# Expert feed-forward in pairs of column steps: weight pieces of 2 row tiles by 1024 columns, scatter into the T and Y banks

## The chip, the core and the metric

The kernel runs on one core of a Trainium2 chip. The metric is the device time of one execution in microseconds. The kernel before takes 1410.08 us (median of 3 runs, 1409.67 to 1410.91).

## What is computed

The program is a two-layer encoder trunk for 256 tokens of width 1024, all in float32. The first layer is a Fourier mixer and a dense SwiGLU; the second is neighbourhood attention and a top-2-of-8 expert SwiGLU. The change touches only the experts:

```python
def expert_block(args):            # xb: the tokens routed to expert e
    xb, e = args
    return (jax.nn.silu(xb @ w_gate[e]) * (xb @ w_up[e])) @ w_down[e]
# w_gate, w_up: 8 x 1024 x 3584;  w_down: 8 x 3584 x 1024
y = ys[dest] * g_sorted[:, None]
out = jnp.zeros((T, D)).at[tok_sorted].add(y)
```

## The kernel before

**Split products.** Each float32 product is made of three matmuls of a reduced type: a number is written as hi + lo, and `three` (L1059) issues hi*hi, hi*lo and lo*hi. Weights come from HBM in pieces of 1 MB (128 partitions by 2048 values, `PIECE`). SyncE (SP) issues one DMA for each into one of 7 raw buffers (`load`, L305), as soon as VectorE (DVE) is done with the buffer's last content. ScalarE (ACT) copies the piece to `w_hi` (`split_hi`, L394), DVE subtracts to `w_lo` (`split_lo`, L671), and TensorE (PE) multiplies (12 matmuls of 512 columns for a piece: three for each of its 4 blocks of 128 by 512). There are only three `w_hi`/`w_lo` buffers (`SPLIT`), so ACT may split piece j+3 only when PE has ended piece j, which PE tells by the semaphore `piece_used`.

**An expert** has 42 pieces. Its hidden width of 3584 is worked in 7 steps of 512 columns (`STEPS`). For each step: gate, 2 pieces of 4 row tiles by 512 columns, into a PSUM bank G[c % 2] (`columns`, L1393); up, 2 pieces, into U[c % 2]; then the down product of the step before, 2 pieces, into the two Y banks (`down`, L1421). ACT takes the Silu of G (`silu`, L597), DVE multiplies it by U (`hidden`, L944), PE transposes the result in four blocks into T[c % 2] (`hidden_transposes`, L1411), and ACT and DVE make hi and lo of it (`hidden_hi`, L603, `hidden_rest`, L951). The function `expert_pieces` (L95) writes the order of the pieces out by hand, and `expert` of ACT (L617) and of DVE (L978) walk through that list: at piece j they first do the small work that hangs on it, then split piece j+3. An engine works strictly in this order.

**Around an expert.** While the last pieces of expert E run, PE gathers the tokens of expert E+1 (`gather`, L1372, 8 matmuls into G[1] and U[1]) and transposes them (`transpose_tokens`, L1384). Then it runs the two pieces of the next expert's first gate step (`first_gate`, L1405), and only then the scatter of expert E: 8 matmuls (L1480, L1481) into T[0], G[1], T[1] and U[1], which DVE adds to h (`add_result`, L968, L974). Experts 0 to 6 are one hardware loop (`Fori`) on each engine, with the same instructions in each round; the eighth stands behind it. In the loop each round of ACT begins at piece 1 of the list, and the first activation of the round is the Silu of step 0.

Of the kernel before, what the change touches and what calls it, by code (L numbers as in the profile page):

```python
# [30 lines left out]
KD = D // P  # L31
# [61 lines left out]

STEPS = FFE // BANK
def expert_pieces():  # L95

    order = []
    for c in range(STEPS):
        order += [("gate", c, 0), ("gate", c, 1), ("up", c, 0), ("up", c, 1)]
        if c:  # L100
            order += [("down", c - 1, 0), ("down", c - 1, 1)]
    order += [("down", STEPS - 1, 0), ("down", STEPS - 1, 1)]
    return order, {x: j for j, x in enumerate(order)}
# [10 lines left out]
def expert_source(ewg, ewu, ewd, e, j):  # L114

    kind, c, half = EXPERT[j]
    v = {"gate": ewg, "up": ewu, "down": ewd}[kind][0].rearrange("e (k p) n -> p (e k) n", p=P)
    if kind == "down":
        return v[:, bass.ds(e * (FFE // P) + (BANK // P * c + KROW * half), KROW), :], KROW, D
    return v[:, bass.ds(e * KD + KH * half, KH), BANK * c:BANK * (c + 1)], KH, BANK  # L120


def trunk(nc, x, norm_mix, norm_ffn, w_in, w_out, w_qkv, w_o, ffg, ffu, ffd, router_w, router_b,
# [149 lines left out]
    def has_before(j, E, back):  # L273

        return E is not None or j >= back


    TY = [T[0], T[1], Y[0], Y[1]]
# [112 lines left out]
    def _(act):  # L391
# [205 lines left out]
        def silu(E, c):  # L597
            act.wait_ge(piece_used, piece(AT["gate", c, 1], E))
            if c != 1:
                act.wait_ge(e_hid, E * STEPS + max(c - 1, 0))  # L600
            nc.scalar.activation(silu_g[c % 2][:], G[c % 2][:], ACT.Silu).then_inc(e_silu, 1)
# [15 lines left out]
        def expert(E, ahead):  # L617

            for j, (kind, c, half) in enumerate(EXPERT):
                if j < AHEAD - SPLIT:  # L620
                    continue
                if (kind, half) == ("gate", 1):
                    silu(E, c)
                    if c:
                        hidden_hi(E, c - 1)
                if (kind, c, half) == ("up", STEPS - 1, 1) and ahead:
                    gather_copy(E + 2)
                if (kind, c, half) == ("down", STEPS - 2, 0):
                    if ahead:
                        gather_hi(E + 2)  # L630
                    hidden_hi(E, STEPS - 1)
                if (kind, c, half) == ("down", STEPS - 1, 1):
                    result_hi(E)
                if ahead or j + SPLIT < PER_EXPERT:
                    split_hi(j + SPLIT, E)
            if ahead:
                for j in range(PER_EXPERT + SPLIT, PER_EXPERT + AHEAD):
                    split_hi(j, E)
# [22 lines left out]
    def _(dve):  # L661
# [282 lines left out]
        def hidden(E, c):  # L944
            dve.wait_ge(e_silu, E * STEPS + (c + 1))
            dve.wait_ge(piece_used, piece(AT["up", c, 1], E))
            if c != 1:
                dve.wait_ge(e_hidT, E * STEPS + max(c - 1, 0))
            nc.vector.tensor_tensor(hid[c % 2][:], U[c % 2][:], silu_g[c % 2][:], ALU.mult).then_inc(e_hid, 1)
# [18 lines left out]
        def add_result(E, e):  # L968
            for b in range(NB):
                for q in range(2):  # L970
                    dve.wait_ge(e_scatter, NB * (2 * E + q) + b + 1)
                    part = h[:, b, BANK * q:BANK * (q + 1)]
                    src = T[q] if b == 0 else (G, U)[q][1]
                    last = nc.vector.scalar_tensor_tensor(out=part, in0=src[:], scalar=mo["weight"][:, b, bass.ds(e, 1)],  # L974
                                                          in1=part, op0=ALU.mult, op1=ALU.add)
                last.then_inc(e_added, 1)

        def expert(E, sweep, ahead):  # L978

            e = E - NE if sweep else E  # L980
            for j, (kind, c, half) in enumerate(EXPERT):
                if j < AHEAD - SPLIT:
                    continue
                if (kind, half) == ("gate", 1) and c:
                    hidden_rest(E, c - 1)
                if (kind, half) == ("up", 1):
                    hidden(E, c)
                    if c == 0:
                        next_selection(E, e, sweep, ahead)
                    if c == STEPS - 1 and ahead:  # L990
                        gather_copy(E + 2)
                if (kind, c, half) == ("down", STEPS - 2, 0):
                    if ahead:
                        gather_lo(E + 2)
                    hidden_rest(E, STEPS - 1)
                if (kind, c, half) == ("down", STEPS - 1, 1):
                    result_rest(E)
                if ahead or j + SPLIT < PER_EXPERT:
                    split_lo(j + SPLIT, E)
# [51 lines left out]
    def _(pe):  # L1051
# [340 lines left out]

        def columns(E, kind, c, bk):  # L1393
            for half in range(2):
                j = AT[kind, c, half]
                ready(j, E)
                if (kind, c) == ("gate", 0):
                    pe.wait_ge(e_xlo, 2 * E + half + 1)
                wh, wl = parts(j, E, KH)
                for k in range(KH):  # L1400
                    kk = KH * half + k
                    last = three(bk[:], mo["xg_hi"][:, kk], mo["xg_lo"][:, kk], wh[:, k], wl[:, k], kk == 0, kk == KD - 1)
                last.then_inc(piece_used, 1)

        def first_gate(E):  # L1405

            pe.wait_ge(e_silu, E * STEPS)
            columns(E, "gate", 0, G[0])

        def expert(E, ahead):  # L1410
# [29 lines left out]

            for c in range(STEPS):
                if c:
                    if c >= 2:
                        pe.wait_ge(e_silu, E * STEPS + (c - 1))
                    columns(E, "gate", c, G[c % 2])
                    hidden_transposes(c - 1)
                if c != 1:
                    pe.wait_ge(e_hid, E * STEPS + max(c - 1, 0))
                columns(E, "up", c, U[c % 2])
                if c == 0:  # L1450
                    pe.wait_ge(e_added, NB * E)
# [3 lines left out]
                    last.then_inc(e_selT, 1)  # L1455
                if 1 <= c < STEPS - 1:
                    down(c - 1, 0)
                    down(c - 1, 1)

            pe.wait_ge(e_hid, E * STEPS + (STEPS - 1))  # L1460
            if ahead:
                pe.wait_ge(e_sel, E + 2)
                gather()
            down(STEPS - 2, 0)
            if ahead:
                transpose_tokens(E + 2)
            hidden_transposes(STEPS - 1)
            down(STEPS - 2, 1)
            down(STEPS - 1, 0)
# [5 lines left out]
            for q in range(2):  # L1475
                pe.wait_ge(e_ylo, 2 * E + 1 + q)
                for b in range(NB):
                    cs = slice(BANK * q, BANK * (q + 1))
                    bk = T[q] if b == 0 else (G, U)[q][1]
                    nc.tensor.matmul(bk[:], mo["selT"][:, b], mo["y_hi"][:, cs], start=True, stop=False)  # L1480
# [66 lines left out]
```

## Time and profile before

| | us |
|---|---|
| median of 3 runs | 1410.08 |
| the execution that was profiled | 1411.13 |
| its span, first to last instruction | 1409.3 |
| one expert in the loop, from the timeline | 122.4 |
| PE busy in the span | 1388.9 |
| DVE busy in the span | 1127.1 |
| ACT busy in the span | 926.1 |

The span is the time between the first and the last instruction; the profiled execution's own time is 1.8 us longer. PE is the engine of the matmuls; its records overlap (one record is 0.39 us long, and the next starts 0.23 us after it), so the start-to-start time is what a matmul costs. On ACT and DVE, too, an instruction starts some 0.1 us before the record of the one ahead of it ends.

### The profile page before, as it was taken

To read this page: it belongs to the slowest core of one execution; us is meant where nothing else is said; L and a number is where in the kernel's file an instruction comes from. 1 tells how busy PE (TensorE), PEld (TensorE's weight loads), DVE (VectorE), ACT (ScalarE), POOL (GpSimd) and SP (SyncE) were. 2 spreads that over 40 slices of the span, in tenths; PEclk is the share of its full clock that TensorE was granted. 3 is DMA by queue.
4 is the path that set the end of the run, shared out by engine and by line. 5 is a ranking of instruction groups with operands and counts; after the bars stand their busy time and mean duration, and the time that the engine had idled before them with its cause. 6 is when DMAs were issued, how large, how long until landed. Compare 5 with 4: busy or idle time off the path is not lost.

```text
span 1409.3 us, 17766 instructions
## 1 busy us (share of the span) xinstructions
PE 1388.9 (99%) x6511; PEld 1151.1 (82%) x6511; DVE 1127.1 (80%) x811; ACT 926.1 (66%) x760; POOL 20.0 (1%) x29
## 2 busy tenths in 40 slices
PE   9999999999979999999999999999999999999997
PEld 8888888787868888888888888888888888888885
DVE  6455666655668889888988988898898889889887
ACT  6353444444656777777777777777777777777774
POOL 0000000000030000000000000000000000000000
PEclk9999999999989999999999999999999999999999
DMA  9367775563148999999999999999999999999992
GB/s 356 132 179 221 220 202 179 172 198 109 32 140 313 361 375 340 359 377 354 356 362 375 334 362 374 357 357 376 366 329 377 363 354 350 368 375 333 372 375 90
DMA packets 191689, 420.10 MB, mean 298 GB/s; under 512 B 19168, under 2 KB 21344, under 8 KB 191648
## 3 DMA queue, kind: packets, MB, share of 16 engines
q1 hardware_dynamic: 178432, 415.00, 81.9%
q10 hardware_dynamic: 12784, 3.26, 1.7%
q0 software_dynamic: 432, 1.28, 0.3%
q8 instruction: 27, 0.44, 0.1%
q14 instruction: 14, 0.11, 0.0%
HBM read 418.47 MB, written 1.05 MB: 298 GB/s over the span
## 4 chain that ended last, share of the span: by engine, by line
PE 97%; DVE 1%; ACT 1%; DMA 1%; issue 0%; POOL 0%; POOLq 0%; SPq 0%; DVEq 0%; ACTq 0%
PE bank_G L1061 10%; PE bank_G L1063 10%; PE bank_G L1062 10%; PE bank_U L1061 10%; PE bank_U L1063 10%; PE bank_U L1062 10%; PE bank_Y L1061 8%; PE bank_Y L1063 8%; PE bank_Y L1062 8%; PE bank_T L1418 2%; PE bank_G L1310 1%; PE bank_T L1061 1%; PE bank_T L1063 1%; PE bank_T L1062 1%; PE bank_T L1321 1%; PE bank_G L1379 1%
## 5 line engine op out<-in xcount | busy, mean ns | idle before, releaser
L674 DVE TENSOR_TENSOR w_lo<-raw,w_hi 128x2048 fp32r<-128x2048 f32 x390 | 888.0, 2290 | 197.7 <-ACT w_hi L400 197.6
L400 ACT ACTIVATE w_hi<-raw 128x2048 fp32r<-128x2048 f32 x390 | 748.2, 1919 | 284.3 <-PE bank_U L1063 102.1
L1061 PE MATMUL bank_Y<-w_hi,hidT_hi 128*128 128x512 f32 x492 | 192.3, 391 | 0.0
L1063 PE MATMUL bank_Y<-w_hi,hidT_lo 128*128 128x512 f32 x492 | 191.6, 389 | 0.0
L1062 PE MATMUL bank_Y<-w_lo,hidT_hi 128*128 128x512 f32 x492 | 191.4, 389 | 0.0
L1061 PE MATMUL bank_U<-w_hi,xg_hi 128*128 128x512 f32 x448 | 179.1, 400 | 0.0
L1061 PE MATMUL bank_G<-w_hi,xg_hi 128*128 128x512 f32 x448 | 175.7, 392 | 0.7 <-DVE w_lo L674 0.5
L1063 PE MATMUL bank_U<-w_hi,xg_lo 128*128 128x512 f32 x448 | 175.0, 391 | 0.0
L1063 PE MATMUL bank_G<-w_hi,xg_lo 128*128 128x512 f32 x448 | 174.8, 390 | 0.0
L1062 PE MATMUL bank_G<-w_lo,xg_hi 128*128 128x512 f32 x448 | 174.7, 390 | 0.0
L1062 PE MATMUL bank_U<-w_lo,xg_hi 128*128 128x512 f32 x448 | 174.6, 390 | 0.0
L1063 PEld LDWEIGHTS bank_Y<-w_hi,hidT_lo 128*128 128x128 f32 x492 | 92.3, 188 | 19.4
L1061 PEld LDWEIGHTS bank_Y<-w_hi,hidT_hi 128*128 128x128 f32 x492 | 92.4, 188 | 19.2
L1062 PEld LDWEIGHTS bank_Y<-w_lo,hidT_hi 128*128 128x128 f32 x492 | 92.4, 188 | 18.7
L1061 PEld LDWEIGHTS bank_G<-w_hi,xg_hi 128*128 128x128 f32 x448 | 84.3, 188 | 18.5 <-DVE w_lo L674 0.8
L1063 PEld LDWEIGHTS bank_U<-w_hi,xg_lo 128*128 128x128 f32 x448 | 84.1, 188 | 18.2
L1063 PEld LDWEIGHTS bank_G<-w_hi,xg_lo 128*128 128x128 f32 x448 | 84.4, 188 | 17.7
L1062 PEld LDWEIGHTS bank_G<-w_lo,xg_hi 128*128 128x128 f32 x448 | 84.4, 188 | 17.3
L1062 PEld LDWEIGHTS bank_U<-w_lo,xg_hi 128*128 128x128 f32 x448 | 84.3, 188 | 16.3
L1061 PEld LDWEIGHTS bank_U<-w_hi,xg_hi 128*128 128x128 f32 x448 | 84.2, 188 | 16.0
L1061 PE MATMUL bank_G<-w_hi,act_hi 128*128 128x512 f32 (+1 forms) x176 | 67.4, 383 | 2.8 <-DVE act_lo L699 1.4
L1061 PE MATMUL bank_U<-w_hi,act_hi 128*128 128x512 f32 (+1 forms) x176 | 67.7, 385 | 0.0
(264 smaller groups left out, 1471.1 us busy)
## 6 DMA issues: line engine op xcount, KB each, us to landing
raw<-in_expert_w_gate SPq DMA_DIRECT2D x112, 1024.0 KB, 7.0
raw<-in_expert_w_up SPq DMA_DIRECT2D x112, 1024.0 KB, 7.0
raw<-in_expert_w_down SPq DMA_DIRECT2D x112, 1024.0 KB, 6.8
raw<-in_nat_w_qkv SPq DMA_DIRECT2D x12, 1024.0 KB, 5.1
raw<-in_ffn_w_gate SPq DMA_DIRECT2D x11, 1024.0 KB, 7.9
raw<-in_ffn_w_up SPq DMA_DIRECT2D x11, 1024.0 KB, 6.0
raw<-in_ffn_w_down SPq DMA_DIRECT2D x11, 1024.0 KB, 5.2
raw<-in_fourier_w_in SPq DMA_DIRECT2D x4, 1024.0 KB, 11.5
```

The source lines that it names most:

```text
L400: nc.scalar.activation(w_hi[w][:], raw[s][:], ACT.Copy).then_inc(hi_made, 1)
L674: nc.vector.tensor_tensor(w_lo[w][:], raw[s][:], w_hi[w][:].bitcast(f32), ALU.subtract).then_inc(lo_made, 1)
L1061: nc.tensor.matmul(out_, xh, wh, start=start, stop=False)
L1062: nc.tensor.matmul(out_, xh, wl, start=False, stop=False)
L1063: return nc.tensor.matmul(out_, xl, wh, start=False, stop=stop)
L1310: last = nc.tensor.matmul(G[i % 2][:, S * n:S * (n + 1)], att["qT"][p0:p0 + HD, m, P * b:P * (b + 1)], att["kT"][p0:p0 + HD, m, :], start= ...
L1321: last = nc.tensor.transpose(T[g % 2][:, o:o + P], hid[g % 2][:, S * n + P * k:S * n + P * (k + 1)], ident[:])
L1379: last = nc.tensor.matmul((G, U)[q][1][:], mo["sel"][:, b], mo[part][:, b, BANK * q:BANK * (q + 1)], start=(n == 0), stop=(n == len(terms) ...
L1418: last = nc.tensor.transpose(T[c % 2][:, P * k:P * (k + 1)], hid[c % 2][:, P * k:P * (k + 1)], ident[:])
```

## The change

The seven steps are grouped as three pairs and a single one (`PAIRED`). A gate or up piece of a pair is 2 row tiles by 1024 columns in place of 4 by 512, so a pair has 4 gate pieces, then 4 up pieces, and each piece feeds both G banks (or both U banks). The number of pieces, their size and the number of matmuls stay. The down products of a pair come after the up pieces of the next one. The first two of the four gate pieces of the first pair stand ahead of the scatter, the other two behind it. The scatter goes into T[0], Y[0], T[1] and Y[1], since G[1] then holds a gate sum. ACT takes the two Silus and the two `hidden_hi` of a pair together behind the last gate piece; DVE does the same with its part. Token transposes stand now between the pieces of down step 4 and the last hidden transposes behind them.

```diff
--- before.py
+++ after.py
@@ -92,14 +92,20 @@
 
 
 STEPS = FFE // BANK
+PAIRED = [(0, 1), (2, 3), (4, 5), (6,)]
+assert sum(PAIRED, ()) == tuple(range(STEPS))
+def parts_of(p):
+
+    return 2 * len(PAIRED[p])
+
 def expert_pieces():
 
     order = []
-    for c in range(STEPS):
-        order += [("gate", c, 0), ("gate", c, 1), ("up", c, 0), ("up", c, 1)]
-        if c:
-            order += [("down", c - 1, 0), ("down", c - 1, 1)]
-    order += [("down", STEPS - 1, 0), ("down", STEPS - 1, 1)]
+    for p in range(len(PAIRED)):
+        order += [(kind, p, part) for kind in ("gate", "up") for part in range(parts_of(p))]
+        if p:
+            order += [("down", c, half) for c in PAIRED[p - 1] for half in range(2)]
+    order += [("down", c, half) for c in PAIRED[-1] for half in range(2)]
     return order, {x: j for j, x in enumerate(order)}
 
 
@@ -117,7 +123,9 @@
     v = {"gate": ewg, "up": ewu, "down": ewd}[kind][0].rearrange("e (k p) n -> p (e k) n", p=P)
     if kind == "down":
         return v[:, bass.ds(e * (FFE // P) + (BANK // P * c + KROW * half), KROW), :], KROW, D
-    return v[:, bass.ds(e * KD + KH * half, KH), BANK * c:BANK * (c + 1)], KH, BANK
+    width = BANK * len(PAIRED[c])
+    tiles = PIECE // width
+    return v[:, bass.ds(e * KD + tiles * half, tiles), BANK * PAIRED[c][0]:BANK * PAIRED[c][0] + width], tiles, width
 
 
 def trunk(nc, x, norm_mix, norm_ffn, w_in, w_out, w_qkv, w_o, ffg, ffu, ffd, router_w, router_b,
@@ -274,6 +282,10 @@
 
         return E is not None or j >= back
 
+
+    def group_of(c):
+
+        return [p for p, steps in enumerate(PAIRED) if c in steps][0]
 
     TY = [T[0], T[1], Y[0], Y[1]]
     STREAM = [TY, TY, TY, [G[0], G[1], U[0], Y[0]]]
@@ -595,7 +607,7 @@
                 nc.scalar.activation(mo["xg_hi"][:, 4 * q:4 * q + 4], four((G, U)[q][1]), ACT.Copy).then_inc(e_xhi, 1)
 
         def silu(E, c):
-            act.wait_ge(piece_used, piece(AT["gate", c, 1], E))
+            act.wait_ge(piece_used, piece(AT["gate", group_of(c), parts_of(group_of(c)) - 1], E))
             if c != 1:
                 act.wait_ge(e_hid, E * STEPS + max(c - 1, 0))
             nc.scalar.activation(silu_g[c % 2][:], G[c % 2][:], ACT.Silu).then_inc(e_silu, 1)
@@ -619,15 +631,16 @@
             for j, (kind, c, half) in enumerate(EXPERT):
                 if j < AHEAD - SPLIT:
                     continue
-                if (kind, half) == ("gate", 1):
-                    silu(E, c)
-                    if c:
-                        hidden_hi(E, c - 1)
-                if (kind, c, half) == ("up", STEPS - 1, 1) and ahead:
+                if kind == "gate" and half == parts_of(c) - 1:
+                    for step in PAIRED[c]:
+                        silu(E, step)
+                    for step in PAIRED[c - 1] if c else ():
+                        hidden_hi(E, step)
+                if (kind, c) == ("up", len(PAIRED) - 1) and half == parts_of(c) - 1 and ahead:
                     gather_copy(E + 2)
+                if (kind, c, half) == ("down", STEPS - 3, 0) and ahead:
+                    gather_hi(E + 2)
                 if (kind, c, half) == ("down", STEPS - 2, 0):
-                    if ahead:
-                        gather_hi(E + 2)
                     hidden_hi(E, STEPS - 1)
                 if (kind, c, half) == ("down", STEPS - 1, 1):
                     result_hi(E)
@@ -943,7 +956,7 @@
 
         def hidden(E, c):
             dve.wait_ge(e_silu, E * STEPS + (c + 1))
-            dve.wait_ge(piece_used, piece(AT["up", c, 1], E))
+            dve.wait_ge(piece_used, piece(AT["up", group_of(c), parts_of(group_of(c)) - 1], E))
             if c != 1:
                 dve.wait_ge(e_hidT, E * STEPS + max(c - 1, 0))
             nc.vector.tensor_tensor(hid[c % 2][:], U[c % 2][:], silu_g[c % 2][:], ALU.mult).then_inc(e_hid, 1)
@@ -970,7 +983,7 @@
                 for q in range(2):
                     dve.wait_ge(e_scatter, NB * (2 * E + q) + b + 1)
                     part = h[:, b, BANK * q:BANK * (q + 1)]
-                    src = T[q] if b == 0 else (G, U)[q][1]
+                    src = (T, Y)[q][b]
                     last = nc.vector.scalar_tensor_tensor(out=part, in0=src[:], scalar=mo["weight"][:, b, bass.ds(e, 1)],
                                                           in1=part, op0=ALU.mult, op1=ALU.add)
                 last.then_inc(e_added, 1)
@@ -981,17 +994,19 @@
             for j, (kind, c, half) in enumerate(EXPERT):
                 if j < AHEAD - SPLIT:
                     continue
-                if (kind, half) == ("gate", 1) and c:
-                    hidden_rest(E, c - 1)
-                if (kind, half) == ("up", 1):
-                    hidden(E, c)
+                if kind == "gate" and half == parts_of(c) - 1 and c:
+                    for step in PAIRED[c - 1]:
+                        hidden_rest(E, step)
+                if kind == "up" and half == parts_of(c) - 1:
+                    for step in PAIRED[c]:
+                        hidden(E, step)
                     if c == 0:
                         next_selection(E, e, sweep, ahead)
-                    if c == STEPS - 1 and ahead:
+                    if c == len(PAIRED) - 1 and ahead:
                         gather_copy(E + 2)
+                if (kind, c, half) == ("down", STEPS - 3, 0) and ahead:
+                    gather_lo(E + 2)
                 if (kind, c, half) == ("down", STEPS - 2, 0):
-                    if ahead:
-                        gather_lo(E + 2)
                     hidden_rest(E, STEPS - 1)
                 if (kind, c, half) == ("down", STEPS - 1, 1):
                     result_rest(E)
@@ -1390,22 +1405,29 @@
                     last = nc.tensor.transpose((G, U)[q][1][:, P * k:P * (k + 1)], mo["xg"][:, P * kk:P * (kk + 1)], ident[:])
                 last.then_inc(e_xT, 1)
 
-        def columns(E, kind, c, bk):
-            for half in range(2):
-                j = AT[kind, c, half]
+        def columns(E, kind, p, parts_now):
+
+            banks = [(G if kind == "gate" else U)[c % 2] for c in PAIRED[p]]
+            tiles = KD // parts_of(p)
+            for part in parts_now:
+                j = AT[kind, p, part]
                 ready(j, E)
-                if (kind, c) == ("gate", 0):
-                    pe.wait_ge(e_xlo, 2 * E + half + 1)
-                wh, wl = parts(j, E, KH)
-                for k in range(KH):
-                    kk = KH * half + k
-                    last = three(bk[:], mo["xg_hi"][:, kk], mo["xg_lo"][:, kk], wh[:, k], wl[:, k], kk == 0, kk == KD - 1)
+                if (kind, p) == ("gate", 0):
+                    pe.wait_ge(e_xlo, 2 * E + tiles * part // KH + 1)
+                wh, wl = parts(j, E, tiles)
+                for k in range(tiles):
+                    kk = tiles * part + k
+                    for q, bk in enumerate(banks):
+                        cs = slice(BANK * q, BANK * (q + 1))
+                        last = three(bk[:], mo["xg_hi"][:, kk], mo["xg_lo"][:, kk], wh[:, k, cs], wl[:, k, cs], kk == 0, kk == KD - 1)
                 last.then_inc(piece_used, 1)
 
+        FIRST = range(AHEAD - SPLIT + 1)
+
         def first_gate(E):
 
             pe.wait_ge(e_silu, E * STEPS)
-            columns(E, "gate", 0, G[0])
+            columns(E, "gate", 0, FIRST)
 
         def expert(E, ahead):
             def hidden_transposes(c):
@@ -1438,33 +1460,36 @@
                         last.then_inc(e_y, 1)
                 last.then_inc(piece_used, 1)
 
-            for c in range(STEPS):
-                if c:
-                    if c >= 2:
-                        pe.wait_ge(e_silu, E * STEPS + (c - 1))
-                    columns(E, "gate", c, G[c % 2])
-                    hidden_transposes(c - 1)
-                if c != 1:
-                    pe.wait_ge(e_hid, E * STEPS + max(c - 1, 0))
-                columns(E, "up", c, U[c % 2])
-                if c == 0:
+            for p, steps in enumerate(PAIRED):
+                if p:
+                    pe.wait_ge(e_silu, E * STEPS + steps[0])
+                    columns(E, "gate", p, range(parts_of(p)))
+                    for c in PAIRED[p - 1]:
+                        hidden_transposes(c)
+                else:
+                    columns(E, "gate", 0, range(len(FIRST), parts_of(0)))
+                pe.wait_ge(e_hid, E * STEPS + steps[0])
+                columns(E, "up", p, range(parts_of(p)))
+                if p == 0:
                     pe.wait_ge(e_added, NB * E)
                     pe.wait_ge(e_sel, E + 1)
                     for b in range(NB):
                         last = nc.tensor.transpose(T[1][:, P * b:P * (b + 1)], mo["sel"][:, b].bitcast(f32), ident[:])
                     last.then_inc(e_selT, 1)
-                if 1 <= c < STEPS - 1:
-                    down(c - 1, 0)
-                    down(c - 1, 1)
-
-            pe.wait_ge(e_hid, E * STEPS + (STEPS - 1))
+                elif p < len(PAIRED) - 1:
+                    for c in PAIRED[p - 1]:
+                        down(c, 0)
+                        down(c, 1)
+
             if ahead:
                 pe.wait_ge(e_sel, E + 2)
                 gather()
-            down(STEPS - 2, 0)
+            down(STEPS - 3, 0)
             if ahead:
                 transpose_tokens(E + 2)
+            down(STEPS - 3, 1)
             hidden_transposes(STEPS - 1)
+            down(STEPS - 2, 0)
             down(STEPS - 2, 1)
             down(STEPS - 1, 0)
             down(STEPS - 1, 1)
@@ -1476,7 +1501,7 @@
                 pe.wait_ge(e_ylo, 2 * E + 1 + q)
                 for b in range(NB):
                     cs = slice(BANK * q, BANK * (q + 1))
-                    bk = T[q] if b == 0 else (G, U)[q][1]
+                    bk = (T, Y)[q][b]
                     nc.tensor.matmul(bk[:], mo["selT"][:, b], mo["y_hi"][:, cs], start=True, stop=False)
                     nc.tensor.matmul(bk[:], mo["selT"][:, b], mo["y_lo"][:, cs], start=False, stop=True).then_inc(e_scatter, 1)
 
```

## Rows read from the trace of the kernel before

**Rows 1.** The page, part 4 (the chain that ended last) and part 5 (line, engine, operation, out<-in | busy us, mean ns of one | idle before, releaser).

```profile
PE 97%; DVE 1%; ACT 1%; DMA 1%; issue 0%; POOL 0%; POOLq 0%; SPq 0%; DVEq 0%; ACTq 0%
...
L674 DVE TENSOR_TENSOR w_lo<-raw,w_hi 128x2048 fp32r<-128x2048 f32 x390 | 888.0, 2290 | 197.7 <-ACT w_hi L400 197.6
L400 ACT ACTIVATE w_hi<-raw 128x2048 fp32r<-128x2048 f32 x390 | 748.2, 1919 | 284.3 <-PE bank_U L1063 102.1
```

**Rows 2.** Windows, one expert's period: busy us of each engine, clock, DMA share, GB/s.

```profile
680.80:803.20 122.40, 122.40 (x560) 101.39 (x559) 109.60 (x69) 91.22 (x63) 0.00 (x0) 1.00 0.98 360
```

**Rows 3.** Timeline of PE at a change of experts: start, us, line, out<-in.

```profile
656.95 0.60 PE L1390 MATMUL bank_G<-ident,xg 128*128 128x128 f32 x4
...
657.82 0.60 PE L1418 MATMUL bank_T<-ident,hid 128*128 128x128 f32 x4
658.18 0.48 PE L1061 MATMUL bank_Y<-w_hi,hidT_hi 128*128 128x512 f32 x1
...
671.71 0.39 PE L1063 MATMUL bank_G<-w_hi,xg_lo 128*128 128x512 f32 x1
...
673.75 0.39 PE L1061 MATMUL bank_U<-w_hi,xg_hi 128*128 128x512 f32 x1
...
678.96 0.39 PE L1063 MATMUL bank_U<-w_hi,xg_lo 128*128 128x512 f32 x1
679.19 0.38 PE L1454 MATMUL bank_T<-ident,sel 128*128 128x128 f32 x2
679.32 0.47 PE L1061 MATMUL bank_G<-w_hi,xg_hi 128*128 128x512 f32 x1
...
684.90 0.60 PE L1418 MATMUL bank_T<-ident,hid 128*128 128x128 f32 x4
```

**Rows 4.** Timeline of ACT, the same stretch.

```profile
672.20 1.28 ACT L601 ACT_TABLE_LOAD   x1 [0.87 <-PE bank_G L1063]
673.49 0.60 ACT L601 ACTIVATE silu_g<-bank_G 128x512 f32<-128x512 f32 x1
673.99 1.91 ACT L400 ACTIVATE w_hi<-raw 128x2048 fp32r<-128x2048 f32 x1
...
685.10 0.60 ACT L601 ACTIVATE silu_g<-bank_G 128x512 f32<-128x512 f32 x1 [0.80 <-PE bank_G L1063]
...
686.11 1.91 ACT L400 ACTIVATE w_hi<-raw 128x2048 fp32r<-128x2048 f32 x1
```

**Rows 5.** Timeline of DVE, the same stretch.

```profile
676.37 4.54 DVE L674 TENSOR_TENSOR w_lo<-raw,w_hi 128x2048 fp32r<-128x2048 f32 x2
680.83 0.69 DVE L949 TENSOR_TENSOR hid<-bank_U,silu_g 128x512 f32<-128x512 f32 x1
681.43 0.41 DVE L958 CAST selT<-bank_T 128x256 fp32r<-128x256 f32 x1
...
682.15 4.49 DVE L674 TENSOR_TENSOR w_lo<-raw,w_hi 128x2048 fp32r<-128x2048 f32 x2
```

**Rows 6.** Groups of instructions on ACT: all table loads.

```profile
L601 ACT ACT_TABLE_LOAD x7 | 9.0, 1283 | 6.0 <-PE bank_G L1063 6.0
...
L448 ACT ACT_TABLE_LOAD x1 | 1.3, 1283 | 2.3 <-issue 2.3
L509 ACT ACT_TABLE_LOAD x1 | 1.3, 1283 | 0.0
```

**Rows 7.** Timeline of PE, two places where it waited for split weights.

```profile
11.51 0.47 PE L1061 MATMUL bank_G<-w_hi,act_hi 128*128 128x512 f32 x1 [0.53 <-DVE w_lo L682]
...
434.49 0.50 PE L1061 MATMUL bank_G<-w_hi,xg_hi 128*128 128x512 f32 x1 [0.53 <-DVE w_lo L674]
```

**Rows 8.** Windows, a stretch in which PE mostly idles (columns as in rows 2).

```profile
408.00:412.00 4.00, 0.95 (x8) 0.47 (x6) 2.17 (x10) 2.88 (x4) 2.97 (x3) 1.00 0.00 0
```

**Rows 9.** The page, part 6: DMA issues, KB each, median us to landing.

```profile
raw<-in_expert_w_gate SPq DMA_DIRECT2D x112, 1024.0 KB, 7.0
...
raw<-in_expert_w_down SPq DMA_DIRECT2D x112, 1024.0 KB, 6.8
```

## The prediction, made before the changed kernel was timed

> **What bounds the kernel now.** I read the chain of waits first: 97% of what ended last is PE [rows 1]. Then the windows: in an expert's period of 122.40 us PE is busy for all 122.40, at a granted clock of 1.00, with DVE at 109.6 and ACT at 91.2 [rows 2]. So the eight experts, some 970 of 1409 us, are a row of matmuls without a gap, and the change can gain only where PE's own work shrinks. It can lose wherever ACT and DVE bring a split piece late. How near they are to late is read from the timelines of the three engines where one expert follows another [rows 3 to 5], and from the groups of table loads [rows 6].
>
> **The slack of the pipeline, before.** A piece is 12 matmuls; 24 take 673.75 to 679.19 = 5.44 us [rows 3], so a piece is 2.72 and a matmul 0.227. When PE starts the last matmul of piece j (call it time 0), its record ends at 0.39, ACT starts some 0.03 later, splits for 1.92, DVE follows 0.04 later for 2.29 [rows 1], and PE could start piece j+3 at about 4.7. It wants it at 0.23 + 5.44 = 5.67. So whatever ACT and DVE do between two splits fits only if it adds less than about 1.0 us to this one chain. Before, a gate end adds a Silu and a hi copy on ACT: 685.10 to 686.11 = 1.01 us [rows 4]; there PE also has four transposes to do, whose 0.5 us make room for it.
>
> **Step 1: the table load and two Silus meet at the end of the first gate (the largest term).** Seven loads of 1.283 us stand before the Silu of step 0, one in each round of the loop and none in the last expert [rows 6]. The round starts with a table that may be either Exp's or Silu's, so the load is written into the loop before its first Silu. Today this costs nothing: it starts at 672.20, behind piece 1 (whose last matmul starts at 671.71), and the scatter of 8 matmuls gives PE another 1.8 us of work before pieces are wanted [rows 3, 4]. After the change piece 3 is the last gate piece, the scatter lies before piece 2, and nothing lies between gate and up. With the clock of the rows shown, pieces 2 and 3 take 673.75 to 679.19, the last matmul starts at 678.96 and ends at 679.35. The load starts 0.10 behind the end, as at 672.20 behind 672.10: 679.44, and 680.73 the first Silu, 681.23 the second (start to start 0.50, 673.49 to 673.99 [rows 4]), 681.73 the split of piece 6, DVE at 683.69, PE at 686.02. PE wants piece 6 at 679.19 + 5.44 = 684.63. Stall 1.39, and a first matmul behind a wait is recorded 0.47 instead of 0.39 long [rows 7]: 1.47 us.
>
> A harder rule stands in the Trainium skill (ScalarE: Activation LUTs, What ACT_TABLE_LOAD costs): it says that a switch costs a drain of about 1380 ns beside the 1283 of the load. The trace disagrees where it can be seen: 672.20 + 1.28 is 673.48 and the Silu starts at 673.49 [rows 4]. ACT was idle before that load, though, so a drain ahead of it would not show; by the page the stall would be 1.4 longer in each round.
>
> **Step 2: the end of the first up group.** DVE now has two `hidden` products and then `next_selection` before it splits. From the start of the last matmul of piece 7: the split of piece 9 occupies DVE from -0.34 (piece 6 ended at -2.33, plus 0.03, 1.92, 0.04), the next DVE instruction starts 2.21 later at 1.87, two products are 1.20 (680.83 to 681.43 for one), selection is 0.72 (681.43 to 682.15), so the split of piece 10 starts at 3.79 and PE has it at 6.12 [rows 5]. PE wants it at 0.23 + 0.13 (two transposes) + 5.58 (24 matmuls behind transposes, 679.32 to 684.90) = 5.94 [rows 3]. Stall 0.18.
>
> **Step 3: the gate ends of the second and third pair.** ACT does two Silus and two hi copies: 4 x 0.50 = 2.0. Chain: 0.42 + 2.0 + 1.92 + 0.04 + 2.29 + 0.04 = 6.71. PE's side: 0.23, eight transposes (0.43 for a group followed by another, half of 656.95 to 657.82, and 0.36 for the last, 657.82 to 658.18) and 5.58: 6.60. Stall 0.11, twice. At the single step ACT has one operation less: no stall. At the other up ends DVE has no selection: 5.4 against 5.67, none. These three small stalls are differences of sums near 6 us and are known to about 0.1 each, from below zero (then they vanish) to 0.25.
>
> **Step 4: PE's own work.** The counts are unchanged: 504 piece matmuls, 38 transposes, 8 gather, 8 scatter. Matmuls that alternate between two banks with the same stationary operand don't run faster: the down products do that today, at the same mean of 389 to 391 ns a record as the G sums. What shrinks is the number of changes from transposes back to matmuls: 24 matmuls behind one take 5.58 rather than 5.44, and four transposes before a matmul are 0.07 shorter than before another group, so a change costs 0.06 net. In a round there are 8 now and 6 afterwards: -0.12.
>
> **Step 5: what costs nothing.** The DMAs: the rows of a gate piece go from 2 KB to 4 KB, as the down pieces have them today, and those land in 6.8 us against 7.0 [rows 9]; they are issued seven pieces ahead, and ACT's waits are for PE [rows 1]. SP issues as many and in the same way. The first split in the loop is now a Copy, and a Copy with no known table loads one too (L448 [rows 6]), which doesn't serve Silu (L509 follows). That second load, 1.28 on ACT before the split of piece 4, is hidden: the split ends at 675.34, and DVE is at the four adds of the scatter until 676.37 [rows 5]; its result is there at 678.7, wanted at 679.19. The scatter into Y instead of G and U moves no wait, because the next down product is 22 us away; the adds end well before. The removed wait on `e_hid` was long met. Tokens' copies get 0.5 us easier on ACT, where there was slack.
>
> **The sum.** A round of experts 2 to 7: 1.47 + 0.18 + 0.22 - 0.12 = 1.75, six times 10.5. Expert 1: its stall of 0.53 at 434.49 [rows 7], which came of the same load standing before the split of piece 4, turns into part of the new one: 1.75 - 0.53 = 1.2. Expert 8, without load and selection, and with three changes fewer: 0.04 + 0.22 - 0.18 = 0.1. Together +11.8 us. On the profiled execution, 1409.3 of span and 1.8 around it, that gives 1422.9; that execution is 1.05 above the median of 1410.08, so the median should come to 1421.9.
>
> **The rivals.**
> *The load leaves the critical place.* It could be put once at the head of the loop, with a table that serves Copy and Silu both. Then the gate end has 0.04 of stall and a round costs 0.04 + 0.18 + 0.22 - 0.12 = 0.32: 1410.1 + 2.5 = 1412.6. Against it: the first Copy of the program took a table that Silu's L509 had to replace, and the load before the Silu is in the loop already.
> *Not slower: the merged transposes pay and nothing stalls.* The same move of the load, and the small stalls of steps 2 and 3 at or below zero. It decides at the third piece behind a gate: if ACT and DVE are 0.2 us quicker there than I count, PE keeps only the gain of fewer changes from transposes to matmuls, 0.06 to 0.14 for each of 17, with the 0.53 of the first expert gone: 1410.1 - 1.5 to 2.9, say 1408.
> *The load costs double.* If ACT must empty itself before a load when it has been busy (step 1: it comes from the split of piece 5 at 678.58, 0.8 earlier), or two loads queue there, another 1.28 in seven rounds: 1421.9 + 9.0 = 1431. The rows show the Silu at once behind the load, which speaks against it. The drain that the Trainium skill names (ScalarE: Activation LUTs, What ACT_TABLE_LOAD costs) is such a mechanism, and by its 1.38 it would be 1431.6.
> *The clock.* A stall of 1.5 us could cost PE its full clock. In the trace 4 us with PE busy for only 0.95 were still granted 1.00 [rows 8], so I give this 2 in 100; with half the clock for 3 us after each stall it would be about 1432.
>
> **How the numbers follow.** The forecast 0.70, the load at the head 0.10, not slower 0.07, double load 0.09, clock 0.02, the rest other. The forecast's own range is 1417 to 1426 (small stalls all zero, 0.4 a round less; or each 0.1 to 0.2 longer). The range for 8 in 10 is 1412.5 to 1427. This measurement can tell about 0.2%, 2.8 us: faster (under 1407.3) 0.03; within 0.13 (the second rival and most of the first); slower 0.84.
>
> **What would show it.** In the profile after: table loads before the Silu of step 0 still 7, and perhaps 7 more before a `w_hi` split at the head of the loop. PE waiting for `w_lo` about 1.4 us once in each round, at the third up piece (columns of U), and 0.1 to 0.2 at three more places; the period 124.1 instead of 122.4. Matmul records still 389 ns, clock still 1.00, DMAs landing near 7 us. If PE has no wait on `w_lo` in the loop, step 1 is wrong; if the wait is 2.7, the double load is right; if gate pieces land much later than 7 us and ACT waits for a DMA, step 5 is.

## The result, and the profile after

The changed kernel takes 1426.41 us (median of 4, 1425.97 to 1426.57), the kernel before in the same comparison 1409.93: a ratio of 1.0115, with an interval of 1.0102 to 1.0127. The forecast was 1421.9, so the direction was right and the loss of 16.5 us is 1.4 times the 11.8 forecast. The time lies 0.4 above the forecast's own range (1417 to 1426) and 0.6 below the upper end of the range for 8 in 10 (1412.5 to 1427). The profiled execution took 1426.57 us, with a span of 1424.8.

The page after, part 4 and part 5 (answers to [rows 1]; the last row is new among the largest waits of PE):

```profile
PE 93%; DVE 3%; ACT 2%; issue 1%; DMA 1%; POOL 0%; DVEq 0%; POOLq 0%; SPq 0%; ACTq 0%
...
L687 DVE TENSOR_TENSOR w_lo<-raw,w_hi 128x2048 fp32r<-128x2048 f32 x390 | 884.3, 2290 | 211.0 <-ACT w_hi L412 210.9
L412 ACT ACTIVATE w_hi<-raw 128x2048 fp32r<-128x2048 f32 x390 | 745.2, 1921 | 312.8 <-PE bank_U L1078 105.7
...
L1076 PE MATMUL bank_U<-w_hi,xg_hi 128*128 128x512 f32 x448 | 179.4, 401 | 8.8 <-DVE w_lo L687 8.6
```

PE's share of the chain fell from 97% to 93%; what came in is DVE and ACT. PE now waits 8.6 us in front of the first matmul of a `bank_U` piece, for `w_lo`. The windows after, one round of the loop (answers to [rows 2]) and the stretch where the first gate begins:

```profile
420.00:424.00 4.00, 3.25 (x16) 2.60 (x17) 3.31 (x4) 1.13 (x2) 0.00 (x0) 1.00 0.72 225
549.90:674.70 124.80, 123.51 (x559) 101.17 (x558) 109.58 (x69) 91.98 (x64) 0.00 (x0) 1.00 0.96 353
```

A round is 124.80 us in place of 122.40, at the same clock of 1.00; the DMA share fell from 0.98 to 0.96, and no wait for a transfer is among those of a round: ACT waits for PE, DVE for ACT, PE for DVE. PE shows 123.51 of 124.80 as busy. That understates the waits: a record of 0.39 us reaches beyond the start of the next matmul, so a wait under 0.16 us beyond the normal 0.23 leaves no idle time at all. Starts have to be read instead. PE between the scatters of experts 2 and 3 (answers to [rows 3]):

```profile
687.17 0.39 PE L1078 MATMUL bank_U<-w_hi,xg_lo 128*128 128x512 f32 x1
688.78 0.50 PE L1076 MATMUL bank_U<-w_hi,xg_hi 128*128 128x512 f32 x1 [1.23 <-DVE w_lo L687]
689.12 0.40 PE L1077 MATMUL bank_U<-w_lo,xg_hi 128*128 128x512 f32 x1
...
694.36 0.38 PE L1477 MATMUL bank_T<-ident,sel 128*128 128x128 f32 x2
...
699.84 0.39 PE L1078 MATMUL bank_G<-w_hi,xg_lo 128*128 128x512 f32 x1
700.25 0.50 PE L1076 MATMUL bank_G<-w_hi,xg_hi 128*128 128x512 f32 x1
...
705.64 0.39 PE L1078 MATMUL bank_G<-w_hi,xg_lo 128*128 128x512 f32 x1
...
711.98 0.39 PE L1078 MATMUL bank_U<-w_hi,xg_lo 128*128 128x512 f32 x1
712.39 0.50 PE L1076 MATMUL bank_U<-w_hi,xg_hi 128*128 128x512 f32 x1
```

There are four places in a round where the next matmul starts late. From 687.17 to 688.78 is 1.61 where 0.23 is normal: a wait of 1.38. 699.84 to 700.25 is 0.41, a wait of 0.18; 711.98 to 712.39 likewise 0.18; a fourth, at the third pair (745.89 to 746.28), is 0.16. Behind each, the first matmul is recorded 0.50 long and the second starts 0.34 later, and the 24 matmuls from 688.78 to 694.36 take 5.58 instead of 5.44. So a wait costs a restart on top of its length, 0.14 here, and it is no smaller behind a short wait. Lined up with the same matmuls of e3 (below), whose round has none of these waits, the round falls behind by 1.53, 0.36, 0.35 and 0.32 at the four places. That is 2.56 in all: 1.90 of waits and 0.66 of restarts, 0.15 to 0.18 each. The round of e3 is 0.14 shorter than the one of the kernel before, which leaves the 2.42 measured.

ACT and DVE around the longest wait (answers to [rows 4] and [rows 5]), and the table loads (to [rows 6]):

```profile
672.18 1.92 ACT L412 ACTIVATE w_hi<-raw 128x2048 fp32r<-128x2048 f32 x1 [0.32 <-PE bank_G L1078]
674.12 1.28 ACT L412 ACT_TABLE_LOAD   x1
675.42 1.92 ACT L412 ACTIVATE w_hi<-raw 128x2048 fp32r<-128x2048 f32 x1
679.43 1.92 ACT L412 ACTIVATE w_hi<-raw 128x2048 fp32r<-128x2048 f32 x1 [2.10 <-PE bank_G L1078]
682.22 1.28 ACT L613 ACT_TABLE_LOAD   x1 [0.86 <-PE bank_G L1078]
683.51 1.09 ACT L613 ACTIVATE silu_g<-bank_G 128x512 f32<-128x512 f32 x2
684.49 5.52 ACT L412 ACTIVATE w_hi<-raw 128x2048 fp32r<-128x2048 f32 x3
```

```profile
686.44 6.70 DVE L687 TENSOR_TENSOR w_lo<-raw,w_hi 128x2048 fp32r<-128x2048 f32 x3 [2.75 <-ACT w_hi L412]
```

```profile
L412 ACT ACT_TABLE_LOAD x7 | 9.0, 1283 | 0.1
L613 ACT ACT_TABLE_LOAD x7 | 9.0, 1283 | 6.1 <-PE bank_G L1078 6.1
```

The load at 682.22 is behind the last gate piece, then come two Silus and the split at 684.49; DVE starts at 686.44 and ends at 688.73, and PE starts at 688.78. The second family of seven loads, before the first split of a round, is there too: 674.12 to 675.40, right behind a split that ends at 674.10, and the next split starts at 675.42. This load begins before the end of the piece that the split waits for, whose last matmul is:

```profile
674.48 0.39 PE L1078 MATMUL bank_G<-w_hi,xg_lo 128*128 128x512 f32 x1
```

The 15.5 us of span by stages, from the first scatter matmul of each expert: up to the first scatter 549.53 before and 549.90 after, +0.4; six rounds from there to 1283.93 and 1298.81, +14.5; the last expert, 114.58 and 115.14, +0.6; behind it nothing. The first stage compares two executions in which the full clock came back at different times. The stretch 420 to 424 has a clock of 1.00 after (the row above) and 0.53 before; in e7 (below), which is the kernel before but for the banks of the scatter, it has 1.00 too. The rows of the kernel before and of e7:

```profile
420.00:424.00 4.00, 3.61 (x11) 2.71 (x11) 2.85 (x4) 1.20 (x2) 0.00 (x0) 0.53 0.74 256
420.00:424.00 4.00, 3.74 (x18) 3.00 (x19) 3.22 (x4) 0.65 (x3) 0.00 (x0) 1.00 0.81 259
```

In e7 the first scatter starts at 547.84. Against that the changed kernel lost 2.1 us in the first stage, and not 0.4.

### The profile page after: what moved, and what is told of

Read it like the earlier page. It is cut to its first block, busy times and chain, and to the rows that moved or that the text cites. A ratio compares the mean times of both kernels' runs of the same rounds, so it can differ in the third digit from the quotient of the medians.

```text
span 1424.8 us, 17736 instructions
## 1 busy us (share of the span) xinstructions
PE 1394.8 (98%) x6511; PEld 1147.7 (81%) x6511; DVE 1126.7 (79%) x811; ACT 931.3 (65%) x767; POOL 20.0 (1%) x29
## 3 DMA queue, kind: packets, MB, share of 16 engines
q0 software_dynamic: 432, 1.28, 0.3%
HBM read 418.47 MB, written 1.05 MB: 294 GB/s over the span
## 4 chain that ended last, share of the span: by engine, by line
PE 93%; DVE 3%; ACT 2%; issue 1%; DMA 1%; POOL 0%; DVEq 0%; POOLq 0%; SPq 0%; ACTq 0%
PE bank_G L1076 10%; PE bank_G L1078 10%; PE bank_G L1077 10%; PE bank_U L1076 9%; PE bank_U L1078 9%; PE bank_U L1077 9%; PE bank_Y L1076 8%; PE bank_Y L1078 8%; PE bank_Y L1077 8%; PE bank_T L1440 2%; DVE w_lo L687 1%; PE bank_G L1325 1%; PE bank_T L1076 1%; PE bank_T L1078 1%; PE bank_T L1077 1%
```

## The experiments

All times are medians; each has the kernel before beside it on the same chip (1410.0 to 1410.1; 1411.3 for e9). A round is the distance of the first scatter matmuls of experts 2 and 3, and the rows shown are of that round.

**e1: the table loaded ahead of the loop.**

```diff
+        nc.scalar.activation(warm[:], half_power[:], ACT.Silu)
         with act.Fori(0, LAST) as E:
             expert(E, True)
```

> The changed kernel, with one small Silu (2 columns) on ACT ahead of the loop, so that the table of Silu is loaded before the loop and every round can do without a load. Theory A (the load before the first Silu makes PE wait 1.38 us in each of 7 rounds, and three small waits of 0.16 to 0.21 with a restart of 0.11 each make the rest): the big wait shrinks to under 0.1 with its restart of 0.11, the three others stay; a round is 123.4 to 123.5 instead of 124.82, the time 1426.4 - 9.4 = 1417.0. Theory B (two Silus and two hi copies in a row are the trouble, with or without a load): the wait at the third up piece stays above 1 us, time above 1424. Theory C (what is left over is from the 4 KB rows of the DMAs or from both banks being written in turn): as A for the big wait, but e3 keeps 0.6 us a round too much.

Measured: 1417.27 us, ratio 1.0055 (1.0039 to 1.0070), round 123.47 (671.55 to 795.02), and no table load is left in the loop. PE at the third up piece (start, length):

```profile
684.02 0.39 PE L1080 MATMUL bank_U<-w_hi,xg_lo 128*128 128x512 f32 x1
684.35 0.50 PE L1078 MATMUL bank_U<-w_hi,xg_hi 128*128 128x512 f32 x1
```

0.33 instead of 0.23: the wait is 0.10, the restart is still there, and the other three waits stayed at 0.18, 0.19 and 0.16. Theory A holds and theory B falls: without the load the two Silus leave a wait of only 0.10, and the load is what costs.

**e2: the small work spread, the load left in place.** ACT's part; DVE's follows it, with `hidden` of a pair's second step one piece behind the last up piece and `next_selection` at the second gate piece of the second pair.

```diff
                 if kind == "gate" and half == parts_of(c) - 1:
-                    for step in PAIRED[c]:
-                        silu(E, step)
-                    for step in PAIRED[c - 1] if c else ():
-                        hidden_hi(E, step)
+                    silu(E, PAIRED[c][0])
+                if (kind, half) == ("up", 0) and len(PAIRED[c]) == 2:
+                    silu(E, PAIRED[c][1])
+                first = parts_of(c) // 2 - 1 if kind == "up" else 0
+                if kind == "up" and c and half in (first, first + 1):
+                    hidden_hi(E, PAIRED[c - 1][half - first])
```

> The changed kernel with its small work spread: of a pair the second Silu one piece later, the hi copies and rests of the hidden transposes at the second and third up piece, the second hidden product one piece later, and the selection of the next tokens two pieces later. The table loads stay where they are. Theory A: the three small waits go (each chain is then under 5.2 us against 5.67 at least), the big one keeps the load and one Silu: 0.1 + 1.28 + 0.5 + 1.92 + 0.04 + 2.29 + 0.04 against 5.28 is 0.89, with restart 1.0; a round 123.3, the time 1409.9 + 7 x 0.9 to 1.0 - 0.5 = 1416. Theory C: 0.6 a round more, 1420.

Measured: 1415.11 us, ratio 1.0035 (1.0022 to 1.0049), round 123.30 to 123.33. PE at the third up piece:

```profile
684.03 0.39 PE L1082 MATMUL bank_U<-w_hi,xg_lo 128*128 128x512 f32 x1
685.16 0.50 PE L1080 MATMUL bank_U<-w_hi,xg_hi 128*128 128x512 f32 x1 [0.74 <-DVE w_lo L689]
```

1.13 instead of 0.23: a wait of 0.90, for which 0.89 was expected, and the only one left in the round.

**e3: both edits.**

> Both edits: the table loaded ahead of the loop, the small work spread. Theory A: no wait of PE for split weights in the loop, a round 122.2 to 122.4, the time 1408.0 to 1409.5: the kernel before, less the 0.53 of the first expert and up to 0.12 a round for fewer changes from transposes back to matmuls. Theory C: a round of 122.9 to 123.0 with no wait shown by the records, time 1414.

Measured: 1407.97 us (11 runs), ratio 0.9986 (0.9977 to 0.9995), round 122.26:

```profile
669.55:791.81 122.26, 122.26 (x559) 101.47 (x558) 109.72 (x69) 89.75 (x61) 0.00 (x0) 1.00 0.98 360
```

PE is busy throughout and the round is 0.14 us shorter than before. Theory C falls: with the same DMAs and the same order of banks as in the changed kernel no loss is left over. The change itself is worth -0.14 a round; all of its loss was in what hung on it.

**e4: the kernel before, with the table loaded ahead of the loop.** The same edit as in e1.

> The kernel before with the same small Silu ahead of the loop and nothing else. Theory A: the load was hidden in each round, since the scatter gives PE 1.8 us of other work there: rounds stay at 122.40, and only the wait of 0.53 of the first expert can go, so the time is 1409.4 (from 1409.9). If the load had a price in the kernel before as well (a rival in which the whole length of the load always counts), 7 x 1.28 = 9 us less: 1401.

Measured: 1409.15 us, ratio 0.9994 (0.9985 to 1.0003), round as before:

```profile
669.43:791.83 122.40, 122.40 (x559) 101.38 (x558) 109.57 (x69) 89.95 (x61) 0.00 (x0) 1.00 0.98 359
```

So the load had no price in the rounds of the kernel before. The 0.9 us that the median is lower fit the first expert's wait of 0.53 [rows 7], which is gone from the trace of e4, but the interval reaches beyond no change.

**e5 and e6: how much slack a gate end has in the kernel before.** A Copy that nobody reads, of 256 and of 1024 columns, behind the Silu at each gate end; its output goes to a free part of `hn`.

```diff
                 if (kind, half) == ("gate", 1):
                     silu(E, c)
+                    nc.scalar.activation(hn[:, 0, :1024].rearrange("p (a n) -> p a n", n=P),
+                                         ident[:].rearrange("p (a n) -> p a n", a=1).to_broadcast([P, 8, P]), ACT.Copy)
```

> The kernel before with one more Copy of 256 columns on ACT behind the Silu at each gate end (7 in an expert, 56 in all), which nobody reads. It measures the slack of the chain from a gate end to the piece three further on. Theory A puts that slack at 0.45 us (chain 0.42 + 0.50 + 0.50 + 1.92 + 0.04 + 2.29 + 0.04 = 5.71 against 6.16): the Copy takes about 0.3, so PE waits for nothing, rounds stay at 122.40, time 1410.0. Rival: the chain has no slack to speak of (PE is fed by the end of each split): 48 gate ends x 0.3 = 14 us more.

> The same with 1024 columns, about 0.95 us on ACT. Theory A: 0.95 is 0.50 over the slack, and each wait costs a restart of 0.11 to 0.14 more: 0.62 at six gate ends of an expert (the first is covered by the scatter), a round 126.1, time 1410 + 8 x 3.7 = 1439.6. If a wait had no restart cost: 0.50 x 48 = 24 us, 1434.

Measured, e5: 1411.00 us, ratio 1.0007 (0.9997 to 1.0016), rounds 122.43 to 122.56, no wait of PE above 0.1. e6: 1437.84 us, ratio 1.0197 (1.0178 to 1.0216), round 125.63 to 125.70. PE in e6 where the third piece behind a gate end begins:

```profile
696.41 0.39 PE L1065 MATMUL bank_U<-w_hi,xg_lo 128*128 128x512 f32 x1
697.12 0.50 PE L1063 MATMUL bank_Y<-w_hi,hidT_hi 128*128 128x512 f32 x1 [0.32 <-DVE w_lo L676]
697.46 0.40 PE L1064 MATMUL bank_Y<-w_lo,hidT_hi 128*128 128x512 f32 x1
```

0.71 instead of 0.23, so a wait of 0.48 (0.48 to 0.51 at all five places of the round). The Copy is recorded 1.05 long and holds ACT for about 0.95, so the slack is 0.45 to 0.47, as worked out. There are five such places, not the six I had expected: behind the last gate the gather comes in between. 5 x (0.49 + 0.14) = 3.15 of the 3.28 by which the round grew. e5's round is longer by some 0.1 us than expected. Lined up with the kernel before, it falls behind by 0.01 to 0.06 at five places, each time over the first few matmuls of a down piece; what delays them stays open.

**e7: the scatter's banks alone,** in the kernel before.

```diff
-                    src = T[q] if b == 0 else (G, U)[q][1]
+                    src = (T, Y)[q][b]
```

> The kernel before with the scatter into T[0], Y[0], T[1], Y[1] and nothing else of the change. Theory A: no wait moves, rounds 122.40, time 1410.0 within 0.5. A rival in which the scatter's banks matter (DVE's adds and the next down product meet in Y) has a round longer by some tenths: 1412 or more.

Measured: 1410.01 us, ratio 1.0000 (0.9990 to 1.0009), rounds 122.40 to 122.46. This part of the change is free.

**e8: e3 with the last hidden transposes joined to the token transposes.**

```diff
                 transpose_tokens(E + 2)
+            hidden_transposes(STEPS - 1)
             down(STEPS - 3, 1)
-            hidden_transposes(STEPS - 1)
```

> The kernel of e3 with the hidden transposes of the last step right behind the token transposes, as in the kernel before, so that PE changes from transposes back to matmuls five times in a round and not six. Theory A: 0.07 a round less, 122.19 against 122.26, in all 0.5 us, 1407.5. A rival (transposes in one run cost more each, so that joining them gives nothing) leaves 122.26.

Measured: 1407.83 us (11 runs), ratio 0.9984 (0.9975 to 0.9993), round 122.18:

```profile
669.46:791.64 122.18, 122.18 (x559) 101.54 (x558) 109.69 (x69) 89.73 (x61) 0.00 (x0) 1.00 0.97 360
```

Another 0.08 a round, in the trace; the medians of e3 and e8 can't tell them apart. The last expert took 0.36 longer than in e3 (1280.36 to 1395.10 against 1280.88 to 1395.26): the joined transposes wait there for DVE's last hidden product (they start 0.54 behind the matmul before them, not 0.23), and this eats most of it. The round is the shortest of the study.

**e9: three table loads at the first gate end.** Two small activations ahead of the first Silu of a round.

```diff
+                    if c == 0 and ahead:
+                        act.wait_ge(piece_used, piece(AT["gate", 0, 3], E))
+                        nc.scalar.activation(warm[:], half_power[:], ACT.Silu)
+                        nc.scalar.activation(warm2[:], half_power[:], ACT.Exp)
```

> The changed kernel with two small activations (2 columns, a Silu and an Exp) ahead of the first Silu of each round, behind the same wait for the last gate piece: three table loads of 1.28 stand there instead of one. Theory A: everything that ACT does there is on PE's path, so the wait of 1.38 grows by 2 x 1.28 and two small activations of 0.19 each, to 4.3; a round 127.8, time 1426.4 + 7 x 2.9 = 1447. The rival of the prediction in which a longer wait costs the clock: the matmuls behind it start at a granted clock of 0.5, and a round is longer by a further 1.5 us or so, 1457.

Measured: 1453.81 us, ratio 1.0304 (1.0274 to 1.0334), rounds 128.31 to 129.53. PE behind the first gate, and windows over it (columns as in [rows 2]):

```profile
694.17 0.39 PE L1084 MATMUL bank_U<-w_hi,xg_lo 128*128 128x512 f32 x1
697.94 0.79 PE L1082 MATMUL bank_U<-w_hi,xg_hi 128*128 128x512 f32 x1 [3.38 <-DVE w_lo L693]
698.53 0.63 PE L1083 MATMUL bank_U<-w_lo,xg_hi 128*128 128x512 f32 x1
698.96 0.63 PE L1084 MATMUL bank_U<-w_hi,xg_lo 128*128 128x512 f32 x1
```

```profile
692.00:696.00 4.00, 2.56 (x12) 1.78 (x10) 0.41 (x1) 3.99 (x5) 0.00 (x0) 1.00 0.89 339
696.00:700.00 4.00, 2.06 (x5) 1.67 (x6) 4.00 (x2) 3.16 (x2) 0.00 (x0) 0.59 0.26 55
700.00:704.00 4.00, 4.00 (x12) 3.12 (x11) 2.29 (x2) 0.53 (x1) 0.00 (x0) 0.55 1.02 403
704.00:708.00 4.00, 4.00 (x21) 3.23 (x20) 2.58 (x2) 3.04 (x2) 0.00 (x0) 1.00 0.95 331
```

694.17 to 697.94 is a wait of 3.54, less than the 4.3 expected, because one of the three loads ran ahead of the wait for the gate piece. It begins before the last matmul of that piece (the fourth line):

```profile
688.38 1.28 ACT L639 ACT_TABLE_LOAD   x1
689.88 1.28 ACT L640 ACT_TABLE_LOAD   x1
691.38 1.28 ACT L615 ACT_TABLE_LOAD   x1
688.73 0.39 PE L1084 MATMUL bank_G<-w_hi,xg_lo 128*128 128x512 f32 x1
```

But behind the wait the matmuls start 0.43 apart instead of 0.23, and the granted clock is 0.59 and 0.55 in two windows, so for most of them at the lower of its two levels, before it is full again. A round is 3.5 to 4.7 us longer than the changed kernel's: 2.2 are the longer wait, and the other 1.3 to 2.5 are what the slow matmuls can account for (0.20 more each, 7 to 13 of them). So theory A alone fails, and the rival of the prediction that I gave 2 in 100 exists, at a wait 2.2 us longer than the change's; no run tests where between the two it sets in. Behind the change's own waits of 1.38 the clock stayed at 1.00.

**e10: the two waits ahead of a Silu in the other order.** In e9 and before the first Copy, where there is one wait, a load ran ahead of it; before the changed kernel's Silu, where there are two, it ran behind the first.

```diff
         def silu(E, c):
-            act.wait_ge(piece_used, ...)
             if c != 1:
                 act.wait_ge(e_hid, E * STEPS + max(c - 1, 0))
+            act.wait_ge(piece_used, ...)
```

> The changed kernel with the two waits ahead of a Silu in the other order: first for the hidden product, which was long ago, then for the last gate piece. In the profile after, the table load of the Silu runs behind the wait for the gate piece, and the one of the first Copy runs ahead of that Copy's only wait. If the load stands between an instruction's first wait and the instruction that carries the last one, it now runs as soon as ACT has split piece 5, in idle time: it starts 0.77 before the gate piece ends, so of its 1.28 some 0.50 stay on the chain. The wait of 1.38 becomes 0.60, a round 124.82 - 0.78 = 124.0, the time 1426.4 - 7 x 0.78 = 1420.9. If the load always stands behind all waits, nothing moves: 124.8 and 1426.4. If it were wholly hidden: 123.47 and 1417.3, as in e1.

Measured: 1420.66 us, ratio 1.0073 (1.0056 to 1.0090), round 123.73. ACT at the first gate end, and PE at the third up piece:

```profile
676.87 1.92 ACT L412 ACTIVATE w_hi<-raw 128x2048 fp32r<-128x2048 f32 x1 [2.10 <-PE bank_G L1078]
678.81 1.28 ACT L613 ACT_TABLE_LOAD   x1
680.10 1.09 ACT L613 ACTIVATE silu_g<-bank_G 128x512 f32<-128x512 f32 x2
```

```profile
684.60 0.39 PE L1078 MATMUL bank_U<-w_hi,xg_lo 128*128 128x512 f32 x1
685.37 0.50 PE L1076 MATMUL bank_U<-w_hi,xg_hi 128*128 128x512 f32 x1 [0.38 <-DVE w_lo L687]
```

The load starts at 678.81, at the end of the split at 678.79, and no longer waits for the gate piece; PE waits 0.54 instead of 1.38. In all the places seen the load stood right ahead of the last wait of its activation, and behind the other one where there were two.

The round came out 0.3 shorter than expected. At the other gate ends the Silu now starts 0.04 behind the end of the gate piece in place of 0.12 (702.62 for a record ending at 702.58, against 706.15 for 706.03), and the waits at the second and third pair shrank from 0.18 and 0.16 to 0.11 and 0.09. That the median still met its 1420.9 is in part luck: the profiled execution took 1419.08, the other three 1.5 to 2.1 more, and the last expert was 0.5 longer than in the changed kernel (115.60), for which I have no cause.

## Why the prediction was right, and by how much its terms were off

*Step 1, the load and two Silus at the first gate end: right.* 1.38 was measured for 1.39; e1 took it away with the load alone, e2 showed the remainder for load and one Silu (0.90 for 0.89), and e4 showed that the load was free before, when the scatter lay behind it. The restart was sized at 0.08 from one record's length; it is 0.14.

*Steps 2 and 3, the small waits: right in place, too small in size.* The waits were 0.18, 0.18 and 0.16 for 0.18, 0.11 and 0.11. The chain at a gate end is 6.75 (705.64 to 712.39) rather than 6.71, and PE wanted the piece at 6.57, not 6.60. The Silu starts 0.12 behind the end of the gate piece where 0.03 was assumed; e10 shows that 0.08 of this goes with the order of its two waits. The term of the sum that failed is the restart: I charged it once in a round, at 0.08, and it comes behind each of the four waits, however short: 0.66 in all. The same 0.14 stood in my own rows, where 24 matmuls behind transposes take 5.58 instead of 5.44, and I counted it for transposes only. The restarts (0.58 too small) and the waits (1.90 for 1.79) make 0.69; less the 0.02 that step 4 gave beyond its forecast, that is the 0.67 by which a round was undersized (2.42 for 1.75). Why a wait brings a restart is not shown by any run.

*Step 4, PE's own work: right.* -0.12 forecast, -0.14 in e3; joining one more change from transposes to matmuls gave another -0.08 in e8. Writing two banks in turn cost and gave nothing that a round shows.

*Step 5: right.* The 4 KB rows, the scatter's banks (e7 alone as well) and the moved copies cost nothing that a round shows: e3 has all of them, and its round is shorter than before. The second load isn't in e3, but in e2 it is, and PE has no wait there at the piece behind it.

*The first and last expert.* For the first, +1.2 was forecast. The +0.4 between the two profiles is so small because the full clock came back earlier in the second; against e7, with a like clock, it is +2.1, so this term was undersized too. For the last, +0.6 was measured for +0.1: its three waits of 0.03, 0.11 and 0.08 are 0.22 for the 0.26 forecast, and the miss is their restarts.

*The rivals.* The load at the head of the loop did not come by itself; made by hand (e1) it gave 1417.3, not the 1412.6 that I had for it. Its round is 1.07 longer than before for a forecast of 0.32, and 0.58 of the 0.75 between them are the same unpriced restarts. "Not slower" came true only with both edits (e3, 1407.97 for a forecast of 1408). The doubled load fell: at the head of the round ACT was busy until 674.10, the load ran from 674.12 and the split followed at 675.42, so 1.32 in all. That is the case which the row before could not show, and it speaks against the drain of about 1380 ns beside the load in the Trainium skill (ScalarE: Activation LUTs, What ACT_TABLE_LOAD costs): with it the split could not have begun before 676.8. In e9, where Silu and Exp take turns, the three loads start 1.50 apart, which is 1.28 of load and 0.20 of the activation between, and again leaves no room for it.

## What to carry to other kernels

When an engine far from busy feeds the busy one through a few buffers, work out the chain from one hand-over to the piece that hangs on it, and the slack there; a regrouping that puts two small works behind one hand-over spends that slack twice. Spread such work over the following pieces and look at what used to cover a table load. A wait of the busy engine costs more than its length: add the restart to each. And look at the order of the waits ahead of an activation that needs a table: put the one that ends last at the end.

## What was not expected of the hardware

- A wait of PE, even one of 0.10 us (e1), cost 0.14 to 0.18 more behind it: the second matmul starts 0.34 after the first instead of 0.23, and the 24 behind a wait took 5.58 instead of 5.44.
- A wait of 3.54 us was followed by matmuls 0.43 apart, with a granted clock of 0.55 to 0.59 in windows of 4 us; waits of 1.38 in the same place were not.
- A table load behind a busy ACT cost 1.32 us from the end of one split to the start of the next, nothing beyond its own length. It ran ahead of the last wait of its activation, so the order of two waits was worth 0.84 us of PE's wait (e10).
